# First block of the first projection loaded, split and multiplied k-tile by k-tile, ten warming products, and the rows of x and the tables queued behind the second block's weights

## What is computed

```python
for layer in range(DEPTH):
    h = rms_norm(x, norm_mix[layer])
    (aq, ak, av, bq, bk, bv, iq, ik, iw, cq, ckv, kr, gate_logits) = jnp.split(
        h @ w_in[layer], split_points, axis=-1)
    ...
    hm = rms_norm(mem, norm_mem[layer])
```

## Time and profile before

| | us |
|---|---|
| median of 3 runs (1881.29 to 1882.37) | 1881.6 |
| the profiled execution, its own time | 1882.23 |
| its span on the core | 1880.9 |
| PE busy in the span | 1866.2 |
| DVE / ACT / POOL busy | 1507.9 / 1275.0 / 101.2 |
| mean traffic | 281 GB/s |

### The profile page before, as it was taken

One profiled execution on the slowest core, in us unless ns is written; L12 is line 12 of the kernel. 1 busy time (PEld: TensorE's weight loads), 2 busy tenths in 40 slices (PEclk: granted clock), 3 DMA queues, 4 the chain that ended last, 5 costly groups with the idle time before them and its releaser, 6 DMA issues.

```text
span 1880.9 us, 27718 instructions
## 1 busy us (share of the span) xinstructions
PE 1866.2 (99%) x9512; PEld 1573.9 (84%) x9512; DVE 1507.9 (80%) x1683; ACT 1275.0 (68%) x1703; POOL 101.2 (5%) x130
## 2 busy tenths in 40 slices
PE   9999999999999999999999999999999999999997
PEld 8887898888888887898888888888888888888886
DVE  5897756555456898665899999999999999999898
ACT  5747544544445747554788888888888888888785
POOL 1020000000000010001430000000000000000000
PEclk9999999999999999999999999999999999999999
DMA  9555653855554454654599999999999999999995
GB/s 333 165 188 169 201 197 125 294 190 191 181 191 138 137 179 157 216 178 137 194 412 396 401 382 368 389 366 402 381 366 389 374 395 381 367 388 389 382 406 187
DMA packets 182990, 530.31 MB, mean 282 GB/s; under 512 B 9248, under 2 KB 18512, under 8 KB 182656
## 3 DMA queue, kind: packets, MB, share of 16 engines
q1 hardware_dynamic: 175568, 504.43, 73.4%
q0 software_dynamic: 4496, 16.82, 2.5%
q10 hardware_dynamic: 2848, 8.03, 1.1%
HBM read 517.56 MB, written 11.56 MB: 281 GB/s over the span
## 4 chain that ended last, share of the span: by engine, by line
PE 93%; DVE 2%; ACT 2%; DMA 1%; SPq 1%; issue 0%; POOL 0%; DVEq 0%; POOLq 0%
PE bank L982 16%; PE bank L969 16%; PE bank L970 16%; PE bank L2044 7%; PE bank L2054 7%; PE bank L2064 7%; PE bank L2087 5%; PE bank L744 4%; PE bank L757 4%; PE bank L753 4%; PE bank L2117 2%; PE bank L1020 1%; DMA raw<-in_w_in 1%; DVE wlo L563 1%; ACT smB L1707 1%; PE bank L2178 1%
## 5 line engine op out<-in xcount | busy, mean ns | idle before, releaser
L563 DVE TENSOR_TENSOR wlo<-raw,whi 128x1024 fp32r<-128x1024 f32 (+3 forms) x958 | 1134.4, 1217 | 197.7 <-ACT whi L560 163.4
L560 ACT ACTIVATE whi<-raw 128x1024 fp32r<-128x1024 f32 (+3 forms) x958 | 996.4, 1058 | 281.3 <-PE bank L982 151.1
L969 PE MATMUL bank<-whi,xg_hi 128*128 128x512 f32 x864 | 338.7, 392 | 0.0
L970 PE MATMUL bank<-whi,xg_lo 128*128 128x512 f32 x864 | 336.4, 389 | 0.0
L982 PE MATMUL bank<-wlo,xg_hi 128*128 128x512 f32 x896 | 276.2, 389 | 0.1
L982 PEld LDWEIGHTS bank<-wlo,xg_hi 128*128 128x128 f32 x896 | 168.1, 188 | 36.0 <-DVE wlo L563 0.8
L969 PEld LDWEIGHTS bank<-whi,xg_hi 128*128 128x128 f32 x864 | 162.3, 188 | 33.0 <-ACT whi L560 0.2
L970 PEld LDWEIGHTS bank<-whi,xg_lo 128*128 128x128 f32 x864 | 162.3, 188 | 32.9
L969 PE MATMUL bank<-whi,hidTw_hi 128*128 128x512 f32 x448 | 175.1, 391 | 0.0
L970 PE MATMUL bank<-whi,hidTw_lo 128*128 128x512 f32 x448 | 174.4, 389 | 0.0
L982 PE MATMUL bank<-wlo,hidTw_hi 128*128 128x512 f32 x448 | 138.0, 389 | 0.0
(11 more groups left out here) (369 smaller groups left out, 2052.2 us busy)
## 6 DMA issues: line engine op xcount, KB each, us to landing
raw<-in_moe_w_gu SPq DMA_DIRECT2D x224, 1024.0 KB, 7.5
raw<-in_moe_w_down SPq DMA_DIRECT2D x112, 1024.0 KB, 7.3
raw<-in_w_in SPq DMA_DIRECT2D x33, 1024.0 KB, 5.1
raw<-in_ffn_w_gu SPq DMA_DIRECT2D x28, 1024.0 KB, 5.2
raw<-in_xa_wkv SPq DMA_DIRECT2D x16, 1024.0 KB, 5.0
raw<-in_ffn_w_down SPq DMA_DIRECT2D x14, 1024.0 KB, 4.9
raw<-in_w_branch SPq DMA_DIRECT2D x12, 1024.0 KB, 5.1
raw<-in_w_out SPq DMA_DIRECT2D x8, 1024.0 KB, 5.1
```

The costliest lines, as they stand in the source:

```text
L560: self.eng.activation(whi[:, ps, 0:size], src, ACT.Copy).then_inc(high_ready, mark(high_ready, "high", p))
L563: self.eng.tensor_tensor(wlo[:, ps, 0:size], src, whi[:, ps, 0:size].bitcast(F32), ALU.subtract).then_inc(low_ready, mark(low_ready, "low" ...
L969: pe.matmul(bank[b][:, :], hi[:, k, 0:P], wh, start=first, stop=False)
L970: pe.matmul(bank[b][:, :], lo[:, k, 0:P], wh, start=False, stop=False)
```

## The change

`xT` and the weights of PA block 0 are loaded one k-tile at a time, 16 loads in turn (128 KB of `xT`, 256 KB of weights) in place of six, each with a semaphore of its own. PA block 0 is cut in 8 pieces of one k-tile in place of 4 of two, so ACT and DVE split, and PE multiplies, by single k-tiles. PE's bias product stands after the sixth k-tile where it stood after the fourth. ACT copies it out after the eighth k-tile's split where it did so after the sixth. There are 10 warming products for 14. The rows of x and the tables are loaded behind unit 2 rather than ahead of it, and ACT and DVE split PA block 1 ahead of the sums of x's squares rather than after them. Nothing changes in layer 1 or from PB on.

```diff
-        per_piece = min(per_unit, PIECE // width)
+        per_piece = min(per_unit, piece // width)
...
+FIRST = (0, "PA", 0)
...
+                          512 if (l, name, b) == FIRST else PIECE)
...
-                    if p == 1:
-                        self.eng.wait_ge(rest_loaded, at("rest of raw 0"))
-                    if off == 0:
+                    if p < KD:
+                        self.eng.wait_ge(first_loaded[p], at("first", p))
+                    elif off == 0:
...
-                    if n == 0:
...
+                    if n < 2:
+                        for k in range(k0, k0 + ku):
+                            sp.dma_start(xT[:, k, :], a["xT"][:, k, :]).then_inc(xT_loaded[k], mark(xT_loaded[k], "xT", k, by=16))
+                            sp.dma_start(raw[:, n, width * (k - k0):width * (k - k0 + 1)], view[:, k - k0]).then_inc(
+                                first_loaded[k], mark(first_loaded[k], "first", k, by=16))
...
-                    if n == 2:
+                    if n == 3:
                         sp.dma_start(x[:, :, :], a["x"].rearrange("b (t p) d -> p (b t) d", p=P)).then_inc(
...
+                    for k in range(KD):
+                        act.wait_ge(xT_loaded[k], at("xT", k))
+                        x_high(k)
+                        sp_.upto(l, "PA", 0, k - 1)
+                    act.wait_ge(bank_full[4], at("bias_vec"))
...
-                    sp_.through(l, "PA", 0)
+                    sp_.through(l, "PA", 1)
                     act.wait_ge(x_loaded, at("x_in"))
...
-            for _ in range(14):
+            for _ in range(10):
...
-                    linear(l, "PA", 0, hT_hi, hT_lo, "xT", last=2)
+                    linear(l, "PA", 0, hT_hi, hT_lo, "xT", last=6)
                     bias_product()
-                    linear(l, "PA", 0, hT_hi, hT_lo, "xT", first=2)
+                    linear(l, "PA", 0, hT_hi, hT_lo, "xT", first=6)
...
-                sp_.through(l, "PA", 0)
+                sp_.through(l, "PA", 0 if l else 1)
                 norm_ms(l, "mix")
```

More of the change, by code:

```diff
@@ L212, with __init__ @@
 class Columns:
-    def __init__(self, name, source, rows, col, width, number, unit0, piece0):
+    def __init__(self, name, source, rows, col, width, number, unit0, piece0, piece=PIECE):
         self.name, self.width, self.number = name, width, number
@@ L240, in product @@
         for b, c in enumerate(range(0, cols, step)):
-            blk = Columns((l, name, b), source, rows, col + c, min(step, cols - c), number, len(units), len(pieces))
+            blk = Columns((l, name, b), source, rows, col + c, min(step, cols - c), number, len(units), len(pieces),
+                          512 if (l, name, b) == FIRST else PIECE)
             blocks[(l, name, b)] = blk
@@ L500, in trunk @@
         x_loaded = sem("x_loaded")
-        xT_loaded = [sem(f"xT{i}_loaded") for i in range(3)]
+        xT_loaded = [sem(f"xT{k}_loaded") for k in range(KD)]
         xT_low = sem("xT_low")
         turned_split = sem("turned_split")
-        rest_loaded = sem("rest_loaded")
+        first_loaded = [sem(f"first{k}_loaded") for k in range(KD)]
         ident_loaded = sem("ident_loaded")
@@ L1376, in straight @@
                     view = src.rearrange("(k p) n -> p k n", p=P)[:, k0:k0 + ku, col:col + width]
-                    if n == 0:
-                        sp.dma_start(xT[:, 0:2, :], a["xT"][:, 0:2, :]).then_inc(xT_loaded[0], mark(xT_loaded[0], "xT", 0, by=16))
-                        sp.dma_start(raw[:, 0, 0:PIECE].rearrange("p (k n) -> p k n", k=2), view[:, 0:2]).then_inc(
-                            raw_loaded[0], mark(raw_loaded[0], "raw", 0, by=16))
-                        sp.dma_start(xT[:, 2:4, :], a["xT"][:, 2:4, :]).then_inc(xT_loaded[1], mark(xT_loaded[1], "xT", 1, by=16))
-                        sp.dma_start(raw[:, 0, PIECE:].rearrange("p (k n) -> p k n", k=2), view[:, 2:4]).then_inc(
-                            rest_loaded, mark(rest_loaded, "rest of raw 0", by=16))
-                        sp.dma_start(xT[:, 4:8, :], a["xT"][:, 4:8, :]).then_inc(xT_loaded[2], mark(xT_loaded[2], "xT", 2, by=16))
+                    if n < 2:
[3 more added lines that the diff above has]
+                                first_loaded[k], mark(first_loaded[k], "first", k, by=16))
                     else:
@@ L1797, in _ @@
                     act.wait_ge(columns_loaded, at("gain columns"))
-                    for i, ks in enumerate(((0, 1), (2, 3), (4, 5, 6, 7))):
-                        act.wait_ge(xT_loaded[i], at("xT", i))
-                        for k in ks:
-                            x_high(k)
-                        sp_.upto(l, "PA", 0, i - 1)
-                        if i == 2:
-                            act.wait_ge(bank_full[4], at("bias_vec"))
-                            act.activation(bias_vec[:, :], bank[4][0:16, 0:384], ACT.Copy).then_inc(
-                                act_freed[4], mark(act_freed[4], "bias_vec_out"))
-                            act.wait_ge(act_freed[4], at("bias_vec_out"))
-                            act.dma_start(bias_dram.ap(), bias_vec[:, :]).then_inc(bias_stored, mark(bias_stored, "bias_stored", by=16))
-                    sp_.through(l, "PA", 0)
+                    for k in range(KD):
[3 more added lines that the diff above has]
+                    act.wait_ge(bank_full[4], at("bias_vec"))
+                    act.activation(bias_vec[:, :], bank[4][0:16, 0:384], ACT.Copy).then_inc(
+                        act_freed[4], mark(act_freed[4], "bias_vec_out"))
+                    act.wait_ge(act_freed[4], at("bias_vec_out"))
+                    act.dma_start(bias_dram.ap(), bias_vec[:, :]).then_inc(bias_stored, mark(bias_stored, "bias_stored", by=16))
+                    sp_.through(l, "PA", 1)
                     act.wait_ge(x_loaded, at("x_in"))
@@ L2714, in _ @@
                 if l == 0:
-                    for i, ks in enumerate(((0, 1), (2, 3), (4, 5, 6, 7))):
-                        for k in ks:
-                            dve.wait_ge(high_copied, at("hi", "xT", k))
-                            dve.scalar_tensor_tensor(hT_lo[:, k, :], xT[:, k, :], gain_cols[:, 0, k:k + 1], hT_hi[:, k, :].bitcast(F32),
-                                                     ALU.mult, ALU.subtract).then_inc(xT_low, mark(xT_low, "lo", "xT", k))
-                        sp_.upto(l, "PA", 0, i - 1)
+                    for k in range(KD):
+                        dve.wait_ge(high_copied, at("hi", "xT", k))
+                        dve.scalar_tensor_tensor(hT_lo[:, k, :], xT[:, k, :], gain_cols[:, 0, k:k + 1], hT_hi[:, k, :].bitcast(F32),
+                                                 ALU.mult, ALU.subtract).then_inc(xT_low, mark(xT_low, "lo", "xT", k))
+                        sp_.upto(l, "PA", 0, k - 1)
                 else:
```

## The result

The changed kernel takes 1885.9 us (median of 17 runs, 1884.34 to 1886.97) against 1881.88 us of the kernel before (17 runs, 1881.2 to 1882.65): 4.0 us slower, a ratio of 1.0020 with a 95% interval of 1.0014 to 1.0027. The profiled execution has a time of 1886.31 and a span of 1884.5 us. PE's busy time is the same as before and the chain still lies on it.

A forecast was written before the change was run, and what follows sets the result against it. The prediction took unit 5's landing in SP's load stream as the bound, with PE's head gain lost behind it. Shorter runs +0.3 and more loads 0 gave 1882.5 us against the profiled 1882.23, as a median 1881.9; range 1880.4 to 1884.0.

The forecast's parts named there:

- What bounds the kernel: Start to the sixteen transposes at 53.86: unit 5's landing bounds, so an earlier PE gains nothing; PE has 1.4 us of slack.
- The loads: SP's load stream in the head: shorter runs cost +0.3 us, ten more loads 0, bounded by -0.3 and 3.6 us.
- +0.3 us for shorter runs: Loads of `xT`: 1 MB in 1 KB runs takes 2.96 us in place of 2.63.
- (a): Start of the head: with single k-tiles PE begins at about 5.6 in place of 7.05, 1.4 us earlier.
- (b): PA block 0: PE's eight k-tiles of 1.4 us follow without a gap and end at 17.4.
- (c): PA block 1: unit 2 lands at 16.8, PE starts at 17.9 in place of 20.89; the head gives 3.0 us.
- (d): Before the twelve transposes: PA's banks wait for POOL's factor at 25.3, giving 27.3 against 29.59; 2.3 us are left.
- (e): Bias table leaves ACT near 14.7; POOL's issues move at most 0.3 us, their traffic is through before unit 5.
- (f): PB block 0's last piece: PE waits 2.1 us for its split behind the memory rows' sums; about 0.2 us left.
- (g): Sixteen transposes: unit 5 at 38.88 + 0.3 carries them with it; the gain left at PB is lost.
- Rival two: Stream of loads: each of ten more loads costs 0.36 us, moving unit 5 and the rest; 1885.5 us, chance 0.10.
- Rival three: PA block 0: PE's clock stays low after a pause behind the warming products, 11 us more there; 1887.1 us, chance 0.05.

The follow-up runs named there:

- the two runs with the wait filled: Products of ones put on PE before PB block 0: 15 in the changed kernel, 1884.68 us; 13 with the sinks load also behind the bias store, 1882.93 us.
- sinks late: Changed kernel with ACT's load of `sinks` issued behind the bias store instead of at 2.61 us: 1884.09 us.
- all but the loads: Changed kernel with the six loads of `xT` and PA block 0 as before, still split and multiplied by single k-tiles: 1884.10 us.
- order edit: Sinks load behind bias store (1884.09 us on the changed kernel), or POOL's factor before its bias loads and DVE's emptying before its splits (1883.20); both: 1882.19.
- four versions that build on them: Both order edits plus: memory rows behind unit 5, 1880.85 us; also ACT's emptying first, 1880.40; six loads, 1880.51; bias loads held until unit 4 landed, 1880.58.

## Why the prediction was wrong, step by step

- **What bounds the kernel.** Right for the kernel before. But the chain was taken as the only thing close to the end. The string by POOL's factor and DVE's splits to PA's banks ended at 26.64 us, 0.1 us before PE wanted them for PB block 0, and the argument gave it slack that it did not have.
- **The loads.** Taken at 0, bounded by -0.3 and 3.6 us. Unit 5 came 1.7 us later (40.58 against 38.91). The sum goes by unit 5, and it let that load move by 0.3 us in all. The lean toward 0 rested on reading the slow stretch as ACT's sinks load mixed in. That reading was right, and the conclusion from it wrong: with sixteen short loads the same tiny runs cost more than twice as much. An effect that was seen in the trace was carried over at its old size. The +0.3 us for shorter runs was not tested alone; by the rates both terms together are some 0.4 us without the sinks.
- **(a)** Right: 5.57 against 5.6. **(b)** Failed: PE waited 1.5 us in the head, and the first k-tile took 2.3 us, its first products at the lower clock (1.22 us for the first two; 0.71 to 1.20 in the other traces with sixteen loads and ten warming products). **(c)** Failed with it: unit 2 at 18.6 for 16.8, PA block 1 at 20.3 for 17.9. The head gave 0.6 us, not 3.0.
- **(d) and (e) are the step that failed most.** (e) let POOL's issues move by at most 0.3 us; they moved by 3.15 (23.33 against 20.18), since the bias table left ACT at 17.57 and not near 14.7. ACT's copy stands behind PE's bias product, and this now behind six k-tiles: every wait of PE in the head goes into it undiminished, and 5.3 us of store, landing and start-up follow. (d) took the factor to be ready at 25.3; it was at 28.5, 3.2 us later. What a queue's order cost was read from the kernel before, in which the bias table was early.
- **(d) also put the wait for PA's banks at the wrong place.** It let PE multiply PB block 0's first piece and wait only before the twelve transposes; but that piece goes into PA block 0's banks, so it could not start before 26.64 us as things stood, and the 2.3 us that (d) kept of the head's gain were 0.1. **(e) also took the bias loads to be through before unit 5 in either case.** Held back by 3.9 us (22.93 to 26.80), with the rest the same, they let unit 5 be split some 5 us earlier.
- **(f)** Did not occur. PE's wait of 3.31 us stood before PB block 0's first piece, and it was longer than the 2.1 us predicted for the last. **(g)** Failed: PE itself carried the transposes, not unit 5.
- **Rival two** came out at 1885.5 us, 0.4 from the measured time, by luck: it had no bias string, no clock and a price for each load, where sixteen took the time of six once the sinks and the bias loads were out of the way. **Rival three** had the right mechanism at the wrong place: the clock was low for part of the first k-tile, and again after the wait before PB block 0. 29.53 to 35.19 is 5.66 us where the kernel before took 4.08 from 26.74 on: 1.6 us in the trace, 1.2 by the two runs with the wait filled.
- **What the runs put in its place.** Slow loads beside the sinks: 1.8 us (sinks late). The factor behind the bias loads and DVE's splits: 2.7 us, of which 1.2 to 1.6 the clock. Together 3.7 of 4.0. The parts do not add up: all but the loads cost 2.1, and the first block's loads, splits and products alone cost 4.0 too, in their trace by waits at other places (before PA block 1, and for the memory rows behind the bias loads). Either order edit gave back only 0.7 of that, so the cause of most of it stays open.

## What to carry to other kernels

When a producer in the head is moved later, follow its product through every queue to the last engine that uses what is queued behind it; here a small table for the attention bias held the factor that emptied PE's banks. Put an instruction that the critical engine waits for ahead of unrelated DMA issues on its queue, and bulk loads that are needed late behind those that are needed soon, as both order edits paid without any change of work (four versions that build on them take 1880.4 to 1880.9 us, 1.1 to 1.7 under the kernel before; their intervals still touch 1). Before counting on slack, look up which buffer the critical engine writes next and who empties it. A small effect seen beside one load pattern is not to be carried over at its size to another.

## What the runs showed of the hardware

- One load of 256 runs of 32 bytes, 8 KB in all, on ACT's queue took SP's stream of short loads from about 338 to 216 GB/s for 5 us (means of seven and eight traces), and its stream of long ones from 370 to 319 (two and three).
- PE's clock fell to its lower level (1.2 GHz) after waits of 1.81, 2.25, 2.27, 2.43 and 3.31 us, and did not after 1.82, 2.07, 2.25, 2.28, 2.33 and 2.81 us in other traces. So the length of such a wait alone doesn't tell; where the clock fell, it cost 1.6 us in the trace of the changed kernel and 1.2 us by the two pairs of kernels with the wait filled, and with it goes the wider spread of the runs.
- Loads issued by POOL from 22.9 us on held back a weight load that SP had issued 6.5 us earlier: its split began at 38.6 us, and by 34 us with them issued from 26.8 us on. The order of issue across queues is not the order of landing.
